# Sample maximum through TensorE, key sums in half pages between the scan's steps, and the low halves of the weights on VectorE

## Time and profile before

| | us |
|---|---|
| median of three runs | 1962.67 |
| the profiled execution | 1960.97 |
| its span | 1959.1 |
| PE busy | 1791.6 (91%) |
| DVE busy | 1110.0 (57%) |
| ACT busy | 604.7 (31%) |
| POOL busy | 1116.0 (57%) |

### The profile page before, as it was taken

How to read it: one execution, slowest core, us unless ns; L and a number is a source line. 1 busy time by engine, 2 the same in 40 slices (tenths; PEclk the granted TensorE clock), 3 DMA queues, 4 the chain that set the end, 5 groups by cost and what they waited for, 6 DMA issues and landing times.

```text
span 1959.1 us, 32040 instructions
## 1 busy us (share of the span) xinstructions
PE 1791.6 (91%) x11898; PEld 1530.8 (78%) x11898; DVE 1110.0 (57%) x1360; ACT 604.7 (31%) x927; POOL 1116.0 (57%) x383
## 2 busy tenths in 40 slices
PE   7899998898988969967999799999999997999997
PEld 5787665565655636646999799999999997999995
DVE  1353656556565563345950389999999999000004
ACT  2021222232222320212322354444444443333333
POOL 1036455465554643004777457777777777677771
PEclk9999898898988978978999989999999999999997
DMA  9766897888989866655656436666666665666651
GB/s 213 180 202 221 282 337 246 297 298 272 322 275 310 288 213 231 196 173 136 180 164 173 129 100 181 174 173 173 172 173 172 173 173 141 171 174 176 175 149 45
DMA packets 537197, 393.44 MB, mean 201 GB/s; under 512 B 23618, under 2 KB 502743, under 8 KB 536535
## 3 DMA queue, kind: packets, MB, share of 16 engines
q1 hardware_dynamic: 404944, 325.07, 55.4%
q10 hardware_dynamic: 132160, 67.11, 12.3%
HBM read 385.47 MB, written 7.02 MB: 200 GB/s over the span
## 4 chain that ended last, share of the span: by engine, by line
PE 55%; issue 14%; DMA 9%; DVE 9%; POOL 8%; SPq 3%; ACT 3%; DVEq 0%; ACTq 0%; POOLq 0%
PE bank L966 12%; PE bank L972 12%; PE bank L967 12%; PE bank L670 11%; DMA work<-in_cache_k 7%; POOL work L583 4%; POOL weights_lo L620 3%; PE bank L638 2%; DMA weight_ring<-in_w_in 2%; ACT weights_hi L1339 1%; PE bank L658 1%; DVE work L1615 1%; SPq L460 1%; SPq L398 1%; PE bank L751 1%
## 5 line engine op out<-in xcount | busy, mean ns | idle before, releaser
L620 POOL TENSOR_TENSOR weights_lo<-weight_ring,weights_hi 128x2048 fp32r<-128x2048 f32 (+1 forms) x166 | 750.5, 4532 | 371.6 <-ACT weights_hi L1339 208.8
L670 PE MATMUL bank<-work,weight_ring 128*128 128x264 f32 x2176 | 555.7, 411 | 7.8 <-DMA weight_ring<-in_w_in 7.3
L670 PEld LDWEIGHTS bank<-work,weight_ring 128*128 128x128 f32 x2176 | 425.1, 201 | 130.8 <-issue 56.7
L583 POOL TENSOR_TENSOR work<-work 128x1024 f32<-128x1024 f32 x128 | 299.2, 2352 | 212.0 <-DMA work<-in_cache_k 139.6
L1339 ACT ACTIVATE weights_hi<-weight_ring 128x2048 fp32r<-128x2048 f32 (+1 forms) x166 | 309.3, 1863 | 332.8 <-PE bank L967 315.6
L966 PE MATMUL bank<-h_hi,weights_hi 128*128 128x264 f32 x1376 | 345.1, 289 | 8.0 <-DVE h_lo L1811 8.0
L967 PE MATMUL bank<-h_lo,weights_hi 128*128 128x264 f32 x1376 | 340.7, 286 | 0.0
L966 PEld LDWEIGHTS bank<-h_hi,weights_hi 128*128 128x128 f32 x1376 | 260.7, 189 | 11.4 <-issue 8.4
L967 PEld LDWEIGHTS bank<-h_lo,weights_hi 128*128 128x128 f32 x1376 | 261.1, 190 | 0.0
L1615 DVE TENSOR_REDUCE work<-work 128x16 f32<-128x1024 f32 x128 | 153.9, 1216 | 165.8 <-POOL work L583 165.5
L972 PE MATMUL bank<-h_hi,weights_lo 128*128 128x264 f32 x1376 | 183.7, 286 | 5.6 <-POOL weights_lo L620 5.6
(11 more groups left out here) (233 smaller groups left out, 2192.0 us busy)
## 6 DMA issues: line engine op xcount, KB each, us to landing
weight_ring<-in_w_up SPq DMA_DIRECT2D x86, 1024.0 KB, 5.6
work<-in_cache_k SPq DMA_DIRECT2D x128, 512.0 KB, 6.0
work<-in_cache_v SPq DMA_DIRECT2D x128, 512.0 KB, 6.6
weight_ring<-in_w_in ACTq DMA_DIRECT2D x60, 1024.0 KB, 12.1
weight_ring<-in_w_down SPq DMA_DIRECT2D x32, 1024.0 KB, 5.9
weight_ring<-in_w_out SPq DMA_DIRECT2D x16, 1024.0 KB, 5.9
weight_ring<-in_w_down SPq DMA_DIRECT2D x16, 704.0 KB, 4.7
weight_ring<-in_w_proj_attn SPq DMA_DIRECT2D x16, 512.0 KB, 4.0
```

Of the source, the lines that this page charges most:

```text
L583: pool.tensor_tensor(page(k_pages, n), page(k_pages, n), q_b[b % 2], ALU.mult).then_inc(kq_ready, 1)
L620: pool.tensor_tensor(w_lo[:, cols].bitcast(F32R), slot3(off % SLOTS, 0, k_tiles).rearrange("p k m -> p (k m)"), w_hi[:, cols], ALU.subtrac ...
L670: last = pe.matmul(bank[n % 2][:, 0:N], slot(n % SLOTS, k), tiles[k], start=(k == 0), stop=(k == len(tiles) - 1))
```

## The change

1. The sample's maximum over partitions no longer runs on POOL. PE transposes the 128x16 partition maxima into the mailbox (`max_rows`), DVE reduces them along the row to 16x1 and multiplies them onto a 16x16 identity (`all_max`), PE multiplies with ones, which puts the 16 maxima on all partitions (`global_max`, mailbox again), and DVE's `shift` reads them from there.
2. The key ring is eight half pages of 256 KB (8 of the 16 pairs each). Loads, products and sums go by halves. DVE sums one page at a time, some inside a scan step, between the two scans and the rotation back (`between`).
3. Consumers of the sample's exponentials come later: value pages of sample i start in the third tile, three to five of them fall in iteration i+1, and `prompt_pv`, `values_to_rows` and the mailbox order move. There are three `score` buffers for two. SP's order is a written list (`K` keys of the next sample, `N` of the one after it, `V` values, `P15` the last page of the sample before).
4. `low` runs on DVE, put before the work of the tile before it, and no longer on POOL.

```diff
-MAIL_ORDER = [("q_rows", 0), ("new_scores", 0), ("k_rows", 0), ("v_rows", 0)]
+MAIL_ORDER = [("q_rows", 0), ("new_scores", 0), ("k_rows", 0)]
 for _i in range(H):
-    MAIL_ORDER += [("combine", _i - 1)] if _i else []
-    MAIL_ORDER += [("sums", _i), ("p_diff", _i), ("attention", _i)]
-    MAIL_ORDER += [("k_rows", _i + 1), ("v_rows", _i + 1)] if _i + 1 < H else []
-MAIL_ORDER += [("kv_sample", 0), ("prompt_states", 0), ("sample_states", 0), ("combine", H - 1)]
+    MAIL_ORDER += [("attention", _i - 1)] if _i else []
+    MAIL_ORDER += [("v_rows", _i), ("max_rows", _i), ("max", _i)] + ([("combine", _i - 1)] if _i else [])
+    MAIL_ORDER += [("sums", _i), ("p_diff", _i)] + ([("k_rows", _i + 1)] if _i + 1 < H else [])
+MAIL_ORDER += [("attention", H - 1), ("kv_sample", 0), ("prompt_states", 0), ("sample_states", 0), ("combine", H - 1)]
...
-        score = [cut(288) for _ in range(2)]
+        score = [cut(288) for _ in range(2)] + [work[:, 12384:12672]]
...
             def load_keys(b, p):
-                wait(sp, k_free, PAGES * b + p - 3)
-                load_page(ck, k_pages, k_in, b, p)
+                n = PAGES * b + p
+                at = sp.value_load(page_no[0:1, n:n + 1], min_val=0, max_val=POOL_PAGES - 1)
+                for e in range(2):
+                    wait(sp, k_free, 2 * n + e - 7)
+                    sp.dma_start(half_page(2 * n + e),
+                                 cache_half(e)[bass.ds(at, 1)].rearrange("o p k -> (o p) k")).then_inc(k_in[(2 * n + e) % 8], 16)
 
...
+                for what in ("K4", "Sk", "P15", "V0", "K5", "V1", "K6", "Sv", "V2", "K7", "V3", "K8", "Q", "V4", "K9", "V5", "K10",
+                             "V6", "K11", "V7", "V8", "K12", "V9", "K13", "V10", "K14", "V11", "K15", "V12", "N0", "N1",
+                             "V13", "N2", "N3", "V14"):
...
                 n = PAGES * b + p
                 if p == 0:
                     pool.wait_ge(qb_in[b % 2], 16 * (b // 2 + 1))
-                pool.wait_ge(k_in[n % 4], 16 * (n // 4 + 1))
-                pool.tensor_tensor(page(k_pages, n), page(k_pages, n), q_b[b % 2], ALU.mult).then_inc(kq_ready, 1)
-
-            def global_max(b):
-                pool.wait_ge(smax_ready, b + 1)
-                wait(pool, ssub_ready, b)
-                pool.partition_all_reduce(small[:, 528:544], small[:, 512:528], P,
-                                          bass.bass_isa.ReduceOp.max).then_inc(gmax_ready, 1)
+                for e in range(2):
+                    pool.wait_ge(k_in[(2 * n + e) % 8], 16 * (n // 4 + 1))
+                    pool.tensor_tensor(half_page(2 * n + e), half_page(2 * n + e), q_b[b % 2][:, e * 512:(e + 1) * 512],
+                                       ALU.mult).then_inc(kq_ready, 1)
 
             fractions(0)
             fractions(1)
             fractions(5)
             for i in range(H):
                 for p in range(PAGES if i + 1 < B else 0):
...
-
-            def low(m, off, k_tiles):
-                pool.wait_ge(wh_ready, m + 1)
-                pool.wait_ge(slot_done, PROJ0 + m - 1)
-                cols = slice((off % 2) * KT * P, (off % 2) * KT * P + k_tiles * P)
-                pool.tensor_tensor(w_lo[:, cols].bitcast(F32R), slot3(off % SLOTS, 0, k_tiles).rearrange("p k m -> p (k m)"),
-                                   w_hi[:, cols], ALU.subtract).then_inc(wl_ready, 1)
...
+                    if (k + 1) % step == 0 and (k + 1) // step in hooks:
+                        hooks[(k + 1) // step]()
                     if (k + 1) % step == 0 and 4 - (k + 1) // step < len(todo):
-                        page_pv(b, todo[len(todo) - 1 - (4 - (k + 1) // step)])
+                        page_pv(*todo[len(todo) - 1 - (4 - (k + 1) // step)])
...
+            def max_rows(b):
+                post(("max_rows", b))
+                pe.wait_ge(smax_ready, b + 1)
+                transpose(bank[2][0:16, 0:P], small[:, 512:528]).then_inc(mail, 1)
+
+            def global_max(b):
+                post(("max", b))
+                pe.wait_ge(gmax_ready, b + 1)
+                pe.matmul(bank[2][:, 0:16], ones[0:16, :], small[0:16, 528:544], start=True, stop=True).then_inc(mail, 1)
+
...
-                t = i + 1
+                t, whole = i + 1, i + 2 < HT
+                tiles = [("v", i + 1)] + ([("u", i + 2)] if whole else []) + [("g", 4 * i + r) for r in range(4)]
...
                 bu(t, 0)
                 bu(t, 1)
                 scores(i, 1, 0)
                 if i:
-                    z_tile(("v", i + 1), i - 1, (13, 14, 15))
-                else:
-                    z_tile(("v", i + 1))
+                    prompt_pv(i - 1)
+                z_tile(tiles[0], before(11, 12, 13) if whole else before(11, 12, 13, 14),
+                       {2: lambda: values_to_rows(i), 3: lambda: max_rows(i)})
                 scores(i, 1, 1)
-                if i + 2 < HT:
-                    z_tile(("u", i + 2), i, (0, 1))
+                z_tile(tiles[1], before(14, 15) if whole else before(15), {2: lambda: global_max(i)})
+                cx(t, 0)
+                bu(t, 2)
+                z_tile(tiles[2], now(0, 1, 2) if whole else now(0, 1, 2, 3), {2: lambda: scores(i, 0, 0)})
+                scores(i, 0, 1)
                 if i:
                     combine(i - 1)
                 denominators(i)
-                cx(t, 0)
-                bu(t, 2)
-                scores(i, 0, 0)
-                z_tile(("g", 4 * i), i, (2, 3, 4) if i + 2 < HT else (0, 1, 2, 3))
-                scores(i, 0, 1)
                 cx(t, 1)
                 bu(t, 3)
-                z_tile(("g", 4 * i + 1), i, (5, 6, 7) if i + 2 < HT else (4, 5, 6))
-                p_diff_rows(i)
+                z_tile(tiles[3], now(3, 4, 5) if whole else now(4, 5, 6, 7))
                 cx(t, 2)
-                if i == H - 2:
+                if not whole:
                     sample_bu()
-                z_tile(("g", 4 * i + 2), i, (8, 9, 10) if i + 2 < HT else (7, 8, 9))
-                prompt_pv(i)
+                z_tile(tiles[4], now(6, 7, 8) if whole else now(8, 9, 10, 11))
                 cx(t, 3)
-                keys_to_rows(i + 1)
-                z_tile(("g", 4 * i + 3), i, (11, 12) if i + 2 < HT else (10, 11, 12))
-                values_to_rows(i + 1)
+                if whole:
+                    z_tile(tiles[5], now(9, 10), {1: lambda: p_diff_rows(i), 3: lambda: keys_to_rows(i + 1)})
...
+            def states(t, p, between=None):
...
+                if between:
+                    between()
                 ch.wait()
...
-                dve.wait_ge(kq_ready, n + 1)
-                if p == 0 and b >= 2:
-                    dve.wait_ge(v_used, PAGES * (b - 1))
-                    dve.wait_ge(mail, MAIL["sums", b - 2] + 1)
-                dve.tensor_reduce(score[b % 2][:, p * 16:(p + 1) * 16], page(k_pages, n).rearrange("p (m d) -> p m d", d=HD),
-                                  AX.X, ALU.add).then_inc(k_free, 1)
+                if p == 0 and b >= 3:
+                    dve.wait_ge(v_used, PAGES * (b - 2))
+                    dve.wait_ge(mail, MAIL["sums", b - 3] + 1)
+                for e in range(2):
+                    dve.wait_ge(kq_ready, 2 * n + e + 1)
+                    dve.tensor_reduce(score[b % 3][:, p * 16 + 8 * e:p * 16 + 8 * e + 8],
+                                      half_page(2 * n + e).rearrange("p (m d) -> p m d", d=HD), AX.X, ALU.add).then_inc(k_free, 1)
 
             def page_max(b):
-                s = score[b % 2]
-                dve.wait_ge(k_free, PAGES * (b + 1))
+                s = score[b % 3]
...
+            def all_max(b):
+                dve.wait_ge(mail, MAIL["max_rows", b] + 1)
+                wait(dve, mail, MAIL["max", b - 1] + 1 if b else 0)
+                dve.tensor_reduce(small[0:16, 544:545], bank[2][0:16, 0:P], AX.X, ALU.max).then_inc(mail_read, 1)
+                dve.wait_ge(mail_read, MAIL["max_rows", b] + 1)
+                dve.tensor_scalar(small[0:16, 528:544], ident[0:16, 0:16], small[0:16, 544:545], None, ALU.mult
+                                  ).then_inc(gmax_ready, 1)
...
+                dve.wait_ge(mail, MAIL["max", b] + 1)
+                s3 = score[b % 3][:, 0:272].rearrange("p (g c) -> p g c", c=16)
+                dve.tensor_tensor(s3, s3, bank[2][:, 0:16].unsqueeze(1).to_broadcast([P, PAGES + 1, 16]),
+                                  ALU.subtract).then_inc(mail_read, 1)
...
-                states(t, 0)
-                shift(i)
-                reduce_pages(b, 0, 1)
-                states(t, 1)
+                states(t, 0, lambda: reduce_page(b, 0))
+                reduce_page(b, 1)
+                all_max(i)
+                states(t, 1, lambda: (shift(i), reduce_page(b, 2)))
+                maxima(i, 1)
+                reduce_page(b, 3)
                 page_sums(i)
-                maxima(i, 1)
-                reduce_pages(b, 2, 3, 4)
-                states(t, 2)
+                reduce_page(b, 4)
```

(20 more changed lines are left out.)

239 lines of the change are left out of this document (125 added, 114 removed).

## The result

The changed kernel takes 1818.80 us (median of 4 runs, 1816.25 to 1823.19) beside 1962.28 (4 runs, 1959.99 to 1966.1): 0.9269 of the time, interval [0.9245, 0.9294]. The forecast was 1874 with a range of 1838 to 1925; the gain is 143 us where 89 were forecast. The profiled execution has a span of 1814.4 us, 144.7 less than before.

The account below looks back on a forecast made before the run. In attention PE waits behind POOL's maximum, with DMA the next bound; the up projection has PE nearly full. Attention -68 (37.5, 5.5, 25) and split products -21 make -89: 1874 on the median's scale, 8-in-10 range 1838 to 1925.

Parts of the forecast that it names:

- the DMA term of an iteration: Attention: keys, values and weights take 71.3 us if never idle, 73.5 at 97%, 74.5 with landing delays; the next bound.
- 66.5 with the new instructions: PE's time per attention iteration: 71.5 us busy, 5.8 less at full clock gives 65.7, with the new instructions 66.5.
- i=0: First attention iteration, with fewer value pages (about 64 us of DMA, 66 of PE): from 73.4 to 68, 5.5 gained.
- Rival B: Attention: DMA gets past the rates taken and PE is the bound at 67.5 us: 131 gained, 1832; chance 0.1.
- i=6: To head 7's scores: waits of 17.7 and 4.8 us, low clock up to 11, less about 2; 25 gained.
- `low` on DVE: Split-precision products: -4 before the first, -9 at the down projection's start, -8 for smaller waits; -21 us in all.
- the 64-column operations: Before the split products: DVE's last two operations, 4.40 and 4.45 us beside POOL, about 0.2 each alone; -8.4.
- The late first low phase: Start of the split products: first `low` behind DVE's wait for nine stores, so tile 0's low phase starts 3 to 6 us late.
- The down start: Start of the down projection: PE's wait from 9.2 to about 2.1 us, with some 2 us at low clock; -9.
- the small waits: PE's waits of 5.6 and 2.4 us elsewhere in the split-precision products go; -8.
- rival of order or small transfers: Attention: ordering or small transfers hold an iteration at 79.5 to 80 us, total 1908; chance 0.2.
- rival D: Attention: page maximum ends after its mailbox hook, PE stands mid-tile, 88 us per iteration, slower at 1984; chance 0.07.

Follow-up runs that it names:

- f: The kernel after, value pages from the fifth on loading only 512 of 1024 columns: 1819.08 us.
- c: The kernel after with the maximum on POOL's all-reduce again, late consumers, half pages and `low` on DVE kept: 1900.92 us.
- d: The kernel before with only the maximum moved to PE and DVE through the mailbox; old order, whole pages, `low` on POOL: 1901.34 us.
- b: The kernel before with only `low` moved to DVE: 1928.23 us.
- a: The kernel after with `low` back on POOL: 1841.47 us.
- k: The kernel after with four whole key pages, and ACT's weight load after the third tile issued behind two mailbox copies: 1824.76 us.
- h: The kernel after with SP's three transposed loads of 86 rows each cut into 80 and 6: 1798.18 us.
- j: The kernel after with the 86-row loads cut into 80 and 6, and the first `low` ahead of DVE's wait for nine stores: 1796.62 us.
- l: The kernel after with 8 extra loads per iteration (i=1 to 5) and ACT's third-tile weight load issued behind two mailbox copies: 1849.97 us.

## Why the prediction was wrong

**The step that failed** is the DMA term of an iteration: "The two shares of that stretch add up to 97%, so 73.5; with landing delays 74.5. DMA, not PE, is the bound that comes next." The iteration took 67.5. Experiment f shows that DMA was not the bound: a fifth of the bytes less changed nothing. The rates of the two queues were near (369 and 278 GB/s predicted, 374 and 282 measured); only the 352 GB/s taken for the keys was low, as their 2-KB rows cost nothing. Wrong was to add the two queues' times end to end and to take the 97% of one stretch as the most they can reach. Their packets overlap (shares of 1.03 after, 1.06 when full), and the stretch of the earlier trace rows wasn't full to its end. Its own windows and slices say so (kernel before; the slices are 500 to 535 us in 40, share in tenths and rate):
```profile
525.00:530.00 5.00, 5.00 (x34) 3.07 (x33) 2.83 (x3) 0.00 (x0) 5.00 (x3) 1.00 1.04 344
530.00:535.00 5.00, 5.00 (x28) 3.44 (x27) 4.86 (x8) 0.84 (x3) 3.00 (x2) 1.00 0.79 247
...
DMA  7999999999997789899999998999999999977867
GB/s 272 335 375 377 410 404 358 314 308 358 290 323 253 287 286 315 288 332 376 354 390 404 396 356 303 372 333 339 357 385 335 325 349 294 386 195 260 308 190 185
```
The share is 1.04 in one part and 0.79 at the end, so 0.97 is the mean of a full and an emptier part. Even in full slices the rate runs from 290 to 410, so a single slice is no ceiling either; it takes a long full stretch of the same mix. With 373 GB/s the term is 63 us, under PE's 66.5. Of the 7.7 us between 74.5 and the 66.8 of the undisturbed iterations, 2.2 are the division by 97%, 1.0 the landing delays, 1.7 the overlap (102.5% of 66.8 is 68.5) and the other 2.8 rates and bytes, the keys' above all.

The next bound is PE at "66.5 with the new instructions", which measured 66.8. That this came within 0.3 us is partly luck: the 71.5 us are those of an 80-us window, and the iteration from 520.60 to 602.47 has 72.7 us busy, so that the clock gave back about 7 us for the 5.8 in the sum. The bound by DMA was 35 us of the 55 missed in i=1 to 5. The 6 us in i=0 (62.1 for 68) aren't its: PE is busy all of the 62.1, where the forecast gave it 66.

**Rival B** (PE bound at 67.5, 1832) was the true mechanism and had a chance of 0.1. It would still have been 13 us high.

**i=6**, 25 of at most 32 expected, gave 37.3: PE is busy 63.23 of 63.50 us there. With the maximum still on POOL (c) the order and half pages give 25 of it, with the maximum alone (d) 5.5. Some of that isn't a gain: between the scores of head 7 and the first split product PE has 55 more matmuls and 4.2 us more of busy time than before (91.3 for 87.1), moved past the mark by the new order. With the value page's 1.2 us that explains most of why that stretch gives back only 1.7 us, though its last wait shrank by 8.4.

**`low` on DVE**, 21 expected, is 31 by experiment b and 22.7 by a. The terms: the 64-column operations -8.4 as worked out (11.9 to 3.4), though a and d show that the change in attention alone gives these too. The late first low phase, priced at 3 to 6 us, was 0.9: the wait for stores ended at 788.25, 4.2 us after the first product, but the high phase ahead of it ran partly at 1.2 GHz (a product every 0.22 us for 0.12) and took 5.7 us itself. The down start -7.4 and the small waits -7.1, near what was predicted; and after the first split product PE is busy 8.2 us less (1005.25 for 1013.43) with the same 7990 matmuls, which I put down to the low clock behind waits; I had counted 2.

**Right**: the gap of 16.4 us, the chain through the mailbox to half a microsecond, DVE's price for `low` and its load in the up loop, the value page that stays, and no rival of order or small transfers. The Trainium skill's rule on transfers under 1 MiB (DMA: Bandwidth & Descriptors, "Bandwidth") asks for at least 1 MiB per DMA for 75% of peak. This trace shows no loss below it, with rings of eight key and four value loads: 256-KB keys and 512-KB values together ran at 374 GB/s of a full share, and halving the pages cost nothing (1818.80 us beside k's 1824.76).

**Where I argued too short.** Two figures beside the sum were loose, without weight for the result: the 80.0 and 72.3 us leave out the landing delays that the 74.5 has, and rival D was to decide from a page maximum 17 us after `bu`, though its condition is the hook at about 9. The forecast gave the half pages no value. They are worth up to 26 us, of which k shows 20 to be ACT's held issue. Why whole pages hold it is argued only: from 360 to 385 us, around the issue that took 5.71, they moved 377 GB/s for 339 in the kernel after, and the runs with extra loads, with issues up to 10.3 us, are near 390 in most slices. The mean share does not tell the cases apart: k has issues up to 5.47 us at 1.02, the kernel after none over 0.41 at 1.03.

## What to carry over

A DMA ceiling is read from a long stretch that is kept full, with the same mix of row sizes, not from the mean of a stretch in which loads wait for free buffers, and not from its best slices; shares of queues may add to more than one, so times per queue don't sum. When DMA is near full, look at how long the issuing instruction itself takes: behind a compute engine's slow DMA issue stand its copies, and moving the issue behind the urgent ones was worth 20 of the 26 us that smaller transfers gave. Two changes that end the same collision must not both be credited with it: run each alone and each on top of the other. Where a small engine operation stands beside a busy POOL, price it alone before calling its engine full.

## What the runs showed of the hardware

- PE's granted clock fell with PE busy. Two windows of 2 us of the kernel after, without a wait of PE in them:
```profile
500.00:502.00 2.00, 2.00 (x7) 1.17 (x6) 0.75 (x2) 0.94 (x5) 1.66 (x2) 0.84 1.05 394
502.00:504.00 2.00, 2.00 (x6) 1.57 (x5) 1.90 (x4) 0.00 (x0) 2.00 (x3) 0.50 1.07 396
```
  PE had just run small products (32 rows, 4 to 256 columns); the same sequence in i=1 to 3 kept 2.4 GHz. It is 1.65 us in each of i=4 and 5 (68.5 for 66.8). In h only i=4 has it, in j again both, so a few us between single executions can be this. What sets it off stays open.
- A DMA issue on ACT's queue took 0.37 us, and up to 10.7 us with a DMA share of 1.06 (l); on SP's queue the second of three transposed loads of 86 rows took 22.7 us, and of 80 rows 0.9.
- A `PARTITION_ALL_REDUCE` of 16 columns, 0.39 us in the busy rows, kept POOL from other work for 15.5 us (c) to 16.4 us (before).
- Beside POOL's `low`, two DVE operations on 64 columns took 4.40 and 4.45 us, and 0.20 and 0.23 between two of them.
